# Encoder step on 8 cores: weight ring by release order, output products in 4+4+8 blocks, loads held behind the last tile's transpose, group 1's input beside xT

## The reference

```python
def run_trunk(x, ...):
    b, c, h = split(x @ w_in)                 # layer 0: gated short convolution
    u = c * h
    mix = (b * conv3(hist ++ u)) @ w_out
    x = layer_norm(ALPHA * x + mix)
    x = layer_norm(ALPHA * x + (silu(x @ w_gate) * (x @ w_up)) @ w_down)
    k, v = split(x @ w_kv)                    # shared K/V, also outputs
    q = x @ w_q                               # layer 1: 64-frame chunks, 576 keys, 16 heads
    mix = softmax(q k^T / sqrt(128) + rel_bias) v @ w_o
    x = layer_norm(ALPHA * x + mix)
    return layer_norm(ALPHA * x + swiglu(x)), conv state, k, v
```

## Time and profile before

| what | value |
|---|---|
| median of 3 runs | 4378.61 us (4370.14 to 4387.35) |
| profiled execution | 4388.21 us, span 4387.1 us on the slowest core (the others 4349.7 to 4377.5) |
| busy: PE, DVE, ACT, POOL | 91%, 27%, 14%, 8% of the span |
| chain that ended last | PE 79%, DMA 12%, ACT 2%, DVE 2% |
| DMA | 446 MB, mean 102 GB/s |

### The profile page before, as it was taken

One profiled execution on the slowest core, in us unless ns is written; L12 is line 12 of the kernel. 1 busy time (PEld: TensorE's weight loads), 2 busy tenths in 40 slices (PEclk: granted clock), 3 DMA queues, 4 the chain that ended last, 5 costly groups with the idle time before them and its releaser, 6 DMA issues.

```text
span 4387.1 us, 56882 instructions; the slowest of 8 cores (4349.7 to 4387.1 us)
## 1 busy us (share of the span) xinstructions
PE 4011.6 (91%) x22432; PEld 2147.4 (49%) x22432; DVE 1185.9 (27%) x1574; ACT 603.6 (14%) x1034; POOL 357.7 (8%) x674
## 2 busy tenths in 40 slices
PE   4997799999996989949999997998777999999998
PEld 2553344454443446525555553566434556555554
DVE  1222422211241013342221114155553221212216
ACT  0110300000021111121000012144212000000002
POOL 1000000010010011001111010000000000000000
PEclk9998899999998989979999998999888999999999
DMA  9665665375557686476645667967646324334252
GB/s 184 87 87 87 111 96 88 56 116 92 80 87 136 111 150 102 85 117 110 114 81 94 111 115 143 201 135 140 127 72 115 68 49 88 68 66 72 45 95 88
DMA packets 255701, 446.22 MB, mean 102 GB/s; under 512 B 133808, under 2 KB 158896, under 8 KB 251088
## 3 DMA queue, kind: packets, MB, share of 16 engines
q0 software_dynamic: 102336, 340.44, 48.5%
q1 hardware_dynamic: 153104, 102.14, 9.3%
HBM read 726.07 MB, written 33.76 MB: 173 GB/s over the span
## 4 chain that ended last, share of the span: by engine, by line
PE 79%; DMA 12%; ACT 2%; DVE 2%; issue 1%; SPq 1%; another core or an unknown queue 1%; POOL 0%; DVEq 0%; ACTq 0%; POOLq 0%
PE PS L307 53%; PE PS L369 21%; DMA xT<-ARENA 5%; PE PS L555 2%; DMA ARENA<-kts 2%; PE PS L663 1%; DMA k_o<-ARENA 1%; DMA ARENA<-w_out 1%; ACT ARENA L349 1%; ACT ARENA L329 1%; SPq L114 1%; DVE X L342 1%; DMA vts<-ARENA 1%; DMA xT<-xt1b 1%
## 5 line engine op out<-in xcount | busy, mean ns | idle before, releaser
L307 PE MATMUL PS<-xT,ARENA 128*128 128x384 bf16 (+3 forms) x13952 | 2421.9, 337 | 176.3 <-DMA xT<-ARENA 91.1
L307 PEld LDWEIGHTS PS<-xT,ARENA 128*128 128x128 bf16 x13952 | 1369.4, 98 | 1228.1 <-issue 203.3
L369 PE MATMUL PS<-ARENA 128*128 128x512 bf16 x5280 | 1158.0, 381 | 90.0 <-DMA ARENA<-w_out 51.2
L369 PEld LDWEIGHTS PS<-ARENA 128*128 128x128 bf16 x5280 | 518.0, 98 | 723.7 <-issue 110.7
L377 DVE SCALAR_TENSOR_TENSOR X<-X,PS 128x1024 f32<-128x1024 f32 x370 | 451.5, 1221 | 667.0 <-PE PS L369 659.6
L404 DVE TENSOR_TENSOR ARENA<-PS,ARENA 128x384 bf16<-128x384 f32 (+2 forms) x308 | 177.5, 577 | 1461.6 <-PE PS L307 1449.5
L401 ACT ACTIVATE ARENA<-PS 128x384 f32<-128x384 f32 (+2 forms) x308 | 155.6, 506 | 2160.3 <-PE PS L307 2159.5
L116 POOL DMA_DIRECT2D ARENA<-w_gu x264 | 139.9, 546 | 1556.9 <-PE PS L369 893.2
L555 PE MATMUL PS<-ARENA,xT 128*128 128x512 bf16 x832 | 193.4, 395 | 51.2 <-DMA xT<-ARENA 46.7
L485 DVE TENSOR_TENSOR ARENA<-PS,ARENA 128x512 f32<-128x512 f32 (+2 forms) x96 | 42.9, 447 | 588.9 <-PE PS L307 584.1
L329 ACT ACTIVATE ARENA<-X,sm 128x2048 bf16<-128x2048 f32 x44 | 88.1, 2002 | 605.4 <-DMA xT<-ARENA 216.0
(11 more groups left out here) (65 smaller groups left out, 784.1 us busy)
## 6 DMA issues: line engine op xcount, KB each, us to landing
ARENA<-w_gu POOLq DMA_DIRECT2D x264, 512.0 KB, 12.2
ARENA<-w_dn POOLq DMA_DIRECT2D x132, 512.0 KB, 7.3
ARENA<-w_in POOLq DMA_DIRECT2D x96, 512.0 KB, 6.6
ARENA<-w_out POOLq DMA_DIRECT2D x32, 512.0 KB, 7.4
ARENA<-w_v POOLq DMA_DIRECT2D x32, 512.0 KB, 16.4
ARENA<-w_k POOLq DMA_DIRECT2D x32, 512.0 KB, 10.7
X<-xr SPq DMA_DIRECT2D x13, 1024.0 KB, 17.4
y_o<-X SPq DMA_DIRECT2D x9, 1024.0 KB, 3.9
```

What stands on the lines that cost most here:

```text
L307: S.op("pe", lambda: nc.tensor.matmul(bank(b, n), wsl(slot, 128 * k, 128), xT[:, k, c0:c0 + n], start=(k == 0), stop=(k == KC - 1)), reads ...
L369: S.op("pe", lambda: nc.tensor.matmul(bank(q0 + cs), r_ap(G, j, c, 128), wsl(slots[i], 512 * cs, 512), start=(i == 0), stop=(i == nk - 1)) ...
```

## The change

The ring takes a 14th slot (`oST`, used for w_o alone). A load goes to the allowed slot that PE released first by the program's order, not to the one loaded longest ago. The product with w_out goes in blocks of 4 (rows 12 to 15), 4 (8 to 11) and 8 (0 to 7); w_o in 5 (heads 8 to 12), 3 (13 to 15) and 8. In the first tile of every block `down` goes through the weights one by one, four banks each, and in the other tiles as before. After a LayerNorm with transposes, six loads are issued as before and the seventh waits for the transposes of the last tile. Group 1's columns of tiles 0 to 3 are loaded into the space of the LayerNorm weights during group 0's K/V, and its mixer reads them there; the mixer's own buffers move. At the start one weight goes ahead of `xT`, and `X` comes during the mixer (pieces 4 to 10); six further `X` tiles are loaded after the first quarter of group 0's K/V. A head's transpose is issued after the next head's first step, and so behind `load_head`. An unused identity goes.

```diff
@@ the ring
-    NSLOT = 13
+    NSLOT = 14
-        slot_off = [oRING + 4096 * i for i in range(8)] + [oR + 36864 - 4096 * (i + 1) for i in range(5)]
+        slot_off = [oRING + 4096 * i for i in range(8)] + [oR + 36864 - 4096 * (i + 1) for i in range(5)] + [oST]
+        hold = {"left": None, "keys": []}
+        def released(i):
+            m = -1
+            for k in wkey(i):
+                w, r = S.last_w.get(k), S.readers.get(k, {})
+                if w is not None and w[0][0] == "w" and not r:
+                    return None
+                if w is not None and w[0] == "pe":
+                    m = max(m, w[1])
+                m = max(m, r.get("pe", -1))
+            return m
+        def wload(src, i=None):
+            if i is None:
+                cand = [(released(j), j) for j in sorted(allowed["set"])]
+                i = min(c for c in cand if c[0] is not None)[1]
+            rd = []
+            if hold["left"] is not None:
+                if hold["left"] == 0:
+                    rd, hold["left"] = hold["keys"], None
+                else:
+                    hold["left"] -= 1
+            S.dma("pool", f"w{i}", av(slot_off[i], 2048, BF16), src, reads=rd, writes=ak(slot_off[i], 4096))
...
@@ down
+                order = [(cs, i) for cs in range(4) for i in range(nk)]
+                if s == G["tiles"][0]:
+                    order = [(cs, i) for i in range(nk) for cs in range(4)]
+                for cs, i in order:
...
             if norm:
                 ln_flush(sink)
+                if sink is None:
+                    hold["left"], hold["keys"] = 6, [f"xT:{G['tiles'][-1]}:{q}" for q in range(4)]
...
@@ attention
-                if i == 8:
-                    S.dma("sp", f"at{b}", r_ap(G, h, 0, 1152).rearrange("p (a b) -> p a b", a=9),
+            def stage_t(h):
+                b = h % 2
+                S.dma("sp", f"at{b}", r_ap(G, h, 0, 1152).rearrange("p (a b) -> p a b", a=9),
                           av(oAT[b], 1152, BF16), reads=ak(oAT[b], 2304), writes=r_key(G, h, 0, 1152), transpose=True)
...
                 stage_v(h, i, pts.pop((h, i)))
+                if i == 0 and h > 0:
+                    stage_t(h - 1)
+            stage_t(NH - 1)
...
@@ group 1's input
-        def up(slot, c0, n, b):
+        def up(slot, c0, n, b, side=False):
             for k in range(KC):
+                o = oGB + 1024 * k
+                mv = av(o, 512, BF16) if side else xT[:, k, c0:c0 + n]
...
-                up(slots[j, w], c0, n, b)
+                up(slots[j, w], c0, n, b, side=(g == 1 and c == 1))
...
+        def load_xt(q, side):
+            if side:
+                S.dma("pool", f"xt{4 + q}", av(oGB + 4096 * q, 2048, BF16).rearrange("p (k c) -> p k c", k=4),
+                      xt1b[:, 4 * q:4 * q + 4, :], writes=ak(oGB + 4096 * q, 4096))
+            else:
+                S.dma("pool", f"xt{q}", xT[:, 4 * q:4 * q + 4, xcol(7):xcol(9)], xt1a[:, 4 * q:4 * q + 4, :],
+                      writes=[f"xT:7:{q}", f"xT:8:{q}"])
...
@@ the sequence
+        slots0 = {(0, "c"): wload(w_in[16])}
         for hf, (c0, n) in enumerate([(16 + 384, 512), (0, 400)]):
...
-        for s in range(7):
-            load_x(s, 128 * s)
+        def step0(j, keys):
+            if 4 <= j < 11:
+                s = (3, 4, 5, 6, 0, 1, 2)[j - 4]
+                load_x(s, 128 * s, keys)
+        def after0(cs):
+            load_xt(cs, False)
+            load_xt(cs, True)
+            if cs == 0:
+                for s, row in ((7, 896), (8, 1024), (0, 1152), (1, 1280), (2, 1408), (3, 1536)):
+                    load_x(s, row)
...
-            down(G, [w_out[128 * j:128 * j + 128, :] for j in range(8, 16)], list(range(8, 16)), first=True)
+            down(G, *w_rows(w_out, range(12, 16)), first=True)
+            allowed["set"] |= {10} if g == 0 else {11}
+            down(G, *w_rows(w_out, range(8, 12)), first=False)
...
+        free3 = sorted(range(3), key=released)
+        down(GO, *w_rows(w_o, range(8, 13)), first=True, at=[13] + free3 + [3])
+        allowed["set"] = {4, 5, 6}
+        down(GO, *w_rows(w_o, range(13, 16)), first=False)
+        allowed["set"] = base8 | {8, 9, 10, 11, 13}
+        down(GO, *w_rows(w_o, range(8)), first=False, norm=True)
```

More of the change, by code:

```diff
@@ L358, in ln_flush, with down @@
                 ln["pend"] = None
-        def down(G, srcs, chunks, first, norm=False, sink=None):
-            slots = [wload(s_) for s_ in srcs]
+        def down(G, srcs, chunks, first, norm=False, sink=None, at=None):
+            slots = [wload(s_, at[i] if at else None) for i, s_ in enumerate(srcs)]
             nk = len(slots)
@@ L365, in down @@
                 q0 = next_quad()
[L366 to L372, removed]
+                c = G["rcol"][s]
+                order = [(cs, i) for cs in range(4) for i in range(nk)]
+                if s == G["tiles"][0]:
+                    order = [(cs, i) for i in range(nk) for cs in range(4)]
+                for cs, i in order:
+                    j = chunks[i]
+                    S.op("pe", lambda: nc.tensor.matmul(bank(q0 + cs), r_ap(G, j, c, 128),
+                                                        wsl(slots[i], 512 * cs, 512),
+                                                        start=(i == 0), stop=(i == nk - 1)),
+                         reads=wkey(slots[i]) + r_key(G, j, c, 128), writes=[bk(q0 + cs)], signal=(i == nk - 1))
                 p = ln["n"] % 2
@@ L432, in ffn, with mixer @@
                 base += nb
[L435 to L437 removed]
+        oC, oU, oV = oXB, oXB + 3840, oXB + 7680
+        def mixer(G, slots, step):
             g = G["g"]
@@ L448, in mixer @@
             Ct, Ut, Vt = av(oC, ul, F32), av(oU, ul, F32), av(oV, vl, F32)
-            banks, slots = {}, {}
+            banks = {}
             def mm(j, w, c):
@@ L514, in rest @@
                 conv(j)
[L516 to L528, removed]
+            for j in range(KC):
                 for w in "chb":
@@ L533, in mixer, with kv @@
                 evac_b(j, 0), evac_b(j, 1)
-        def kv(G, mid=None):
+                step(j, wkey(slots[j, "c"]))
+        def kv(G, after):
             g = G["g"]
@@ L613, in kv @@
                     k_head(h)
-                if cs == 2 and mid is not None:
-                    mid()
+                after(cs)
         oA = oGB
@@ L787, in attention, with load_x, w_rows @@
                 stage_v(h, i, pts.pop((h, i)))
[L790 to L798, removed]
+                if i == 0 and h > 0:
[8 more added lines that the diff above has]
+                      writes=[f"xT:7:{q}", f"xT:8:{q}"])
+        def load_x(s, row, after=()):
+            S.dma("sp", f"x{s}", X[:, s, :], xr[row:row + 128, :], reads=after, writes=[f"X:{s}"])
+        def w_rows(w, ks):
+            return [w[128 * j:128 * j + 128, :] for j in ks], list(ks)
         base8 = set(range(8))
+        allowed["set"] = base8 | {8, 9}
+        slots0 = {(0, "c"): wload(w_in[16])}
         for hf, (c0, n) in enumerate([(16 + 384, 512), (0, 400)]):
```

47 lines of the change are left out of this document (12 added, 35 removed).

## The result

Four executions of the changed kernel took 4153.5, 4192.5, 4230.1 and 4519.0 us; in the last two the cores of one die ran at a lower granted clock than the others, and they are left out, as such runs of before are. The ratio to before is **0.953, 95% interval 0.942 to 0.965**. The profiled execution took 4153.5 us (span 4152.5), where that of before took 4388.2: 234.7 us less. Forecast were 251 less on that execution, and 4128 us against the median; the two executions that count have a mean of 4173.0.

A forecast was written before the change was run, and what follows sets the result against it. PE, busy 91% of the span, was taken as the bound, its waits mostly for DMAs. Gains 25 + 71 + 56 + 20.6 + 23 + 28 + 15 + 15 - 3 = 251 us gave 4128 us from the median; range 4083 to 4200, its own 4088 to 4165.

The forecast's parts named there:

- Start: Kernel start: one weight ahead of xT and X late let PE's second product begin earlier; 25 us gained, 22 to 28.
- section 2: Products with w_out and w_o: smaller blocks and a weight-by-weight first tile cover the weight loads; 71 us gained, 65 to 74.
- section 4: Group 1's input loaded early: xt1b waits go, 20.6 us; K/V, jointly with the hold, gains 23, 5 to 36.
- Section 6: Last head: w_o begins with heads 8 to 12, so the wait for its transpose goes; 15 us gained, 13 to 16.
- section 3: Loads held behind the last tile's transpose: xT waits before the gated layers shrink, 56 us gained, 46 to 63; K/V waits shrink too.
- section 5: Attention: issuing a head's transpose behind the next loads lets K come earlier; 28 us gained, 15 to 33.
- section 7: PE clock: fewer restarts at half clock, 2 us per long wait and 0.4 per short; 15 us gained, 8 to 25.
- A: LayerNorm transposes: the hold shortens nothing, late transposes are slow by themselves; 4207 us, chance 0.08.
- C: First tiles: changing bank at each matmul halves PE's clock, costing 158 us; 4286 us, chance 0.05.
- D: Gated layers: the in-order ring stalls at down-block boundaries, 25.6 us each; 4384 us with ten, 4589 with 18; chance 0.03.
- B: Queues fill: K/V and attention give nothing back (23 + 28), the start only 22; 4182 us, chance 0.13.

The follow-up runs named there:

- no hold: The changed kernel without any hold of weight loads behind the last tile's transposes, all else as changed; 4203.0 us.
- gated only: The changed kernel with the hold kept only before the gated layers, not before K/V; 4169.5 us.
- paced: The changed kernel, hold kept, with K/V's V and K weight loads in both groups waiting for earlier V and K stores; 4136.3 us.
- all: Changed kernel plus late X, paced loads in group 1's K/V, w_o behind the last head's V, q weights one head further ahead; 4095.8 us, ratio 0.939.
- the six runs: Six runs with group 1's K/V as in the changed kernel, itself included; that stage took 204.8 to 209.5 us, mean 206.8.
- the run with w_o behind V: The changed kernel with the first w_o load waiting until the last head's V has landed; 4146.5 us.
- The two-block run: The changed kernel with the w_out product in two blocks of eight in place of 4 + 4 + 8; 4187.0 us.

## Why the prediction was right, and where it was not

The sum was 16 us too large on the profiled execution and 45 against the mean of the two (4173.0 for 4128); the range 4088 to 4165 holds the profiled one, 4083 to 4200 both. The direction and the mechanisms of the large terms were right. That the sum came so near is in part luck: the clock gave back 16 us that I had not asked of it, while K/V and the attention fell short by 41.

- **Start, output products, xt1b, the last head's transpose** (sections 1, 2, 4, 6): within 3 us each. In section 2 the reason was half right: the small blocks matter (36 us), the walk weight by weight does not for w_out, only 4.6 us for w_o. The ring's new order was not switched off by itself.
- **Hold before the gated layers** (section 3): 58.5 against 56, and switched off alone 55.4. The transpose is slow because of the loads beside it. 32.9 us stay idle where I said 35.
- **K/V: the step that failed.** I forecast that "K/V goes from 52.6 (46.7 + 5.9) to 30"; the idle time of the two stages went from 57.2 to 56.1. The xT waits did go. But section 3 asked of the held loads only who waits for them late, not whom they meet when they start: in group 1 that is the stores, which I put at nothing and which cost 15 to 26 us by the four runs that ease it (no hold, gated only, paced, all), some 3 less against the mean of the six runs. And section 4 made 18 us of six X tiles, three times the stall of two, but set 8, since the first quarter's stores no longer stand behind any; it was 18.4. Without both, K/V takes 390.5 us in place of 427.7: the 36 us that I had as the good bound were there to be had.
- **Attention** (section 5): the K waits went as forecast, 33.3 us, and new ones came, 9.5 for V, 9.2 for the transpose behind it, 7.1 for w_q. Section 6 let five w_o weights load "during the last head into free slots" and did not ask what they pass. That was 8 us, by the run with w_o behind V. The table's shortfall of 19 us is half the profiled core's own: over six cores the idle time fell by 17.5 of the 28. With the q weights issued a head earlier, in the run of all edits, no w_q wait is left.
- **Clock** (section 7): 31.4 against 15. I priced long waits at 2 us each and short ones at 0.4, but most of it was in stages where PE trickles between landings: 13.0 us of busy time in the attention, 8.7 in w_out, 4.3 in w_o, 6.0 in the second mixer. The two-block run gives one price, 12 us of busy time for 24 us of waits.
- **Rivals.** A and C are refuted by their own runs, D by the absence of any w_gu or w_dn wait. B named half of what happened, and its 4182 lies nearer to 4173.0 than my 4128: K/V gave nothing back, but by two places that can be mended, not because the queues are full.

Section 3 weighed turns between queues and made 9 us of them for a late transpose. The Trainium skill ("DMA: Bandwidth & Descriptors", section "Queues, rings and completion order") has a DMA engine take turns between the queues that it has work for, a packet at a time. The traces agree with that, and not with the 9 us, if what the profile counts as a packet is what takes a turn. Packets and MB while group 0's late transpose flew, first in after (q1 carries the transpose, q0 the loads), then q0 without the hold, where q1 has 2080 again:

```profile
q1 hardware_dynamic: 2080, 0.52, 47.9%
q0 software_dynamic: 144, 0.52, 43.6%
```

```profile
q0 software_dynamic: 1152, 4.19, 83.6%
```

A transpose is 2080 small packets, a load of the same bytes 144, so section 3's equal turns were not equal bytes: all eight loads got through before the transpose ended. As an estimate from these rows, its own 4.3 us and 3.24 for each load make 7.5 for one load (8.31 measured) and 30.2 for eight (30.13 measured; 30.62 in before, beside 1152 packets too). Other late transposes of before and of the run without the hold took up to 5 us less than such a sum, 17.4 to 23.9 beside 819 to 993 packets. No run changed the packets.

Open: that the hold loses in group 1 and gains 7 us in group 0 fits the float32 stores, which only group 1 has, but no run took those stores away. Nor was it settled why pacing both groups cost the attention 10 us. The start, xt1b and the order of a head's transpose were not switched off one by one: their gains are read from the waits that went.

## What to carry to other kernels

Holding loads back moves their traffic, so ask what is in flight when they are let go: here the transposes gained 58 us and small stores lost 20 of it, until the loads were tied to the stores. A store that frees one of four buffers is as urgent as a weight, and a bulk load that nobody needs soon should stand behind it in the queue or be issued late. Waits that let PE trickle cost more than their length: they also lower its clock.

## What the runs showed of the hardware

- A 64 to 256 KB store of K landed after about 30 us beside ten 512 KB loads let go together and after 9 to 16 us when the loads were paced. A transpose of 4.3 us took 8.31 beside one load, 30.13 beside eight.
- Between waits of 1 to 6 us for landings the granted clock of a whole product was 0.90, and 1.00 without them.
